# Feed-forward products of a hybrid two-block network by one level of Strassen's scheme

## The reference

```
u = _rmsnorm(h, norm_ffn_w[l])
hid = jax.nn.silu(u @ w_ffn_gate[l]) * (u @ w_ffn_up[l])      # 2048 -> 5632, twice
h = h + hid @ w_ffn_down[l]                                   # 5632 -> 2048
```

## Time and profile before

| | |
|---|---|
| median of three runs | 3690.56 us (3689.16 to 3692.22) |
| span of the profiled execution | 3688.3 us; the page gives no other time of that execution |
| TensorE busy | 3379.9 us (92%) |
| VectorE, ScalarE, GpSimd busy | 27%, 13%, 3% |
| granted TensorE clock, mean | 0.951 of full speed |
| memory traffic | 598 MB, 162 GB/s |

### The profile page before, as it was taken

One profiled execution on the slowest core, in us unless ns is written; L12 is line 12 of the kernel. 1 busy time (PEld: TensorE's weight loads), 2 busy tenths in 40 slices (PEclk: granted clock), 3 DMA queues, 4 the chain that ended last, 5 costly groups with the idle time before them and its releaser, 6 DMA issues.

```text
span 3688.3 us, 42993 instructions
## 1 busy us (share of the span) xinstructions
PE 3379.9 (92%) x17796; PEld 2888.8 (78%) x17796; DVE 1006.7 (27%) x1555; ACT 469.7 (13%) x751; POOL 126.1 (3%) x89
## 2 busy tenths in 40 slices
PE   6899998899999999889967959999899999998999
PEld 4787787788888777778856847688778888887888
DVE  5357534532310333120254741341110000001000
ACT  2114300000001222110031012211000000000000
POOL 0013300000000000010000000000000000000000
PEclk8999999899999999999977979999999999999999
DMA  9754465665554222334313332133434344342443
GB/s 411 305 213 161 183 259 242 250 250 229 228 207 154 95 102 103 114 114 159 141 65 103 114 123 94 69 133 131 165 137 151 145 159 153 143 159 100 150 156 117
DMA packets 52038, 598.39 MB, mean 162 GB/s; under 512 B 9639, under 2 KB 12214, under 8 KB 13406
## 3 DMA queue, kind: packets, MB, share of 16 engines
q1 hardware_dynamic: 51934, 596.88, 42.5%
HBM read 593.70 MB, written 3.16 MB: 162 GB/s over the span
## 4 chain that ended last, share of the span: by engine, by line
PE 74%; DVE 10%; DMA 9%; issue 2%; DVEq 2%; ACT 2%; SPq 1%; ACTq 0%; POOLq 0%; POOL 0%
PE bank L261 43%; PE bank L273 13%; PE bank L1904 8%; DMA ring<-in_t_mod 8%; DVE E L313 3%; DVE W L1584 2%; PE bank L285 2%; DVE W L1586 1%; PE bank L351 1%; PE aux L1198 1%; PE aux L1153 1%; DVE arena L1422 1%; DVE arena L313 1%; PE aux L833 0%; PE aux L1187 0%
## 5 line engine op out<-in xcount | busy, mean ns | idle before, releaser
L261 PE MATMUL bank<-hT,ring 128*128 128x256 f32 x6144 | 1343.0, 382 | 18.8 <-DVE hT L486 13.9
L261 PEld LDWEIGHTS bank<-hT,ring 128*128 128x128 f32 x6144 | 1175.7, 192 | 183.8 <-issue 20.5
L261 PE MATMUL bank<-arena,ring 128*128 128x256 f32 x3072 | 685.7, 387 | 25.7 <-DVE arena L1885 10.0
L261 PEld LDWEIGHTS bank<-arena,ring 128*128 128x128 f32 x3072 | 595.9, 194 | 112.7 <-issue 28.1
L273 PE MATMUL bank<-hT,ring 128*128 128x256 f32 x2304 | 534.9, 385 | 42.9 <-DMA ring<-in_t_ga 42.9
L273 PEld LDWEIGHTS bank<-hT,ring 128*128 128x128 f32 x2304 | 431.4, 192 | 119.0 <-issue 63.9
L1904 PE MATMUL bank<-arena,ring 128*128 128x256 f32 x1408 | 307.1, 382 | 13.1 <-DVE arena L1930 13.1
L1904 PEld LDWEIGHTS bank<-arena,ring 128*128 128x128 f32 x1408 | 269.5, 192 | 50.6 <-issue 13.5
L377 ACT ACTIVATE arena<-bank 128x512 f32 (+1 forms) x120 | 71.7, 597 | 1411.8 <-PE bank L261 1411.7
L313 DVE SCALAR_TENSOR_TENSOR E<-ring,c_act,E 128x512 f32<-128x512 f32 x240 | 180.2, 751 | 18.5 <-issue 0.6
L1930 DVE TENSOR_TENSOR arena<-arena 128x2816 f32<-128x2816 f32 x4 | 12.1, 3086 | 604.1 <-ACT arena L377 604.1
(11 more groups left out here) (335 smaller groups left out, 1977.7 us busy)
## 6 DMA issues: line engine op xcount, KB each, us to landing
ring<-in_t_mod SPq DMA_DIRECT2D x64, 2048.0 KB, 15.4
ring<-in_t_gate SPq DMA_DIRECT2D x22, 2048.0 KB, 7.7
ring<-in_t_up SPq DMA_DIRECT2D x22, 2048.0 KB, 7.7
ring<-in_t_down SPq DMA_DIRECT2D x32, 1408.0 KB, 5.9
ring<-in_t_out SPq DMA_DIRECT2D x16, 2048.0 KB, 7.8
ring<-in_t_zs SPq DMA_DIRECT2D x16, 2048.0 KB, 7.7
ring<-in_t_gdn SPq DMA_DIRECT2D x12, 2048.0 KB, 7.7
ring<-in_t_u SPq DMA_DIRECT2D x8, 2048.0 KB, 8.3
```

What stands on the lines that cost most here:

```text
L261: last = nc.tensor.matmul(bank[s][:, T * f:T * f + T], w[:, j, P * f:P * f + P], act[:, j, :], start=j == 0, stop=j == kd - 1)
```

## The change

The first two slots (one of gate, one of up) are multiplied as before. Every later gate and up slot, now loaded in turn, and every down slot are multiplied by one level of Strassen's scheme in Winograd's form: a slot's weights are taken as 2x2 blocks (even and odd contraction tile, first and second 128 output columns), the activations as 2x2 blocks (even and odd tile, first and second 128 tokens), and seven products of blocks replace eight. VectorE forms four sums of weight blocks for each slot (`dve_combos`) into one of two sets of rooms (a spare ring place, and the scratch tiles E and W), once the sums of activation blocks (`dve_halves`), and joins the seven products into four result blocks (`dve_joined`). ScalarE copies one product of each of the two banks a slot uses, since VectorE adds it to others in the same bank. Hidden tiles are formed two at a time after each up slot (`dve_hidden`), with their own block sums. The ring has three places in this part. A down product is two output tiles over 44 contraction tiles, loaded in three chunks of 8, 8 and 6 block columns. The loop bodies are six slots. The parts of the diff that matter (the removed functions stand above):

```diff
+        FRING = 3
+        FIRST_FFN = sum(n for _, n in ORDER)
+        HALF = KD // 2
+        PAIRED = KF // 2
+        CHUNKS = [(0, HALF), (HALF, HALF), (2 * HALF, PAIRED - 2 * HALF)]
+        PLAIN, GU = 2, 2 * PAIRED
+        LOOPS_GU, LOOPS_DOWN = (GU - PLAIN) // 6, HALF // 2
+        ffn_slot = [ring[:, (FIRST_FFN + k) % RING, :] for k in range(FRING)]
+        spare_slot = (FIRST_FFN + FRING) % RING
+        combo = [[ring[:, spare_slot, 1024 * q:1024 * q + 1024] for q in range(4)],
+                 [x[:, 1024 * q:1024 * q + 1024] for x in (E, W) for q in range(2)]]
...
+        h_1, h_2, h_3, h_4 = (room(3 * PAIRED * P + HALF * P * k, HALF * P) for k in range(4))
+        f_flat = w_gate[:].rearrange("p j n -> p (j n)")
+        f_up, f_two = f_flat[:, 0:512], f_flat[:, 512:640]
+        f_keep = [w_beta[:].rearrange("p j n -> p (j n)"), rstd[:]]
...
+        def weights(n, half=HALF):
+            return ffn_slot[n % FRING][:, 0:4 * half * P].rearrange("p (j a f n) -> p a f j n", a=2, f=2, n=P)
+        def sums(n, half=HALF):
+            return [x[:, 0:half * P].rearrange("p (j n) -> p j n", n=P) for x in combo[n % 2]]
+        def sp_ffn(sp):
+            def load(n, from_, half=HALF):
+                sp.dma_start(ffn_slot[n % FRING][:, 0:4 * half * P], from_).then_inc(f_in[n % FRING], 16)
+            gu, down = t["t_gu"], t["t_down"]
+            for n in range(FRING):
+                wait_old(sp, (FIRST_FFN + n) % RING)
+                load(n, gu[n])
+            with sp.Fori(0, LOOPS_GU - 1) as i:
+                for r in range(6):
+                    sp.wait_ge(f_done, 6 * i + r + 1)
+                    load(FRING + r, gu[ds(6 * i + FRING + r, 1)].rearrange("o p n -> (o p) n"))
+            for n in range(FRING + 6 * (LOOPS_GU - 1), GU):
+                sp.wait_ge(f_done, n - FRING + 1)
+                load(n, gu[n])
+            with sp.Fori(0, LOOPS_DOWN) as i:
+                for r in range(6):
+                    first, half = CHUNKS[r % 3]
+                    sp.wait_ge(f_done, 6 * i + GU + r - FRING + 1)
+                    at = slice(4 * first * P, 4 * (first + half) * P)
+                    load(GU + r, down[ds(2 * i + r // 3, 1), :, at].rearrange("o p n -> (o p) n"), half)
+        def pe_products(n, pair, half, x, halves, begins=True, ends=True):
+            w, (s1, s2, s3, s4), (x1, x2, x3, x4) = weights(n, half), sums(n, half), halves
+            first, second = bank[2 * pair], bank[2 * pair + 1]
+            for out, group in ((first, ((w[:, 0, 0], x[0][0]), (w[:, 1, 0], x[1][0]), (s2, x2))),
+                               (second, ((s1, x1), (s3, x3), (s4, x[1][1]), (w[:, 1, 1], x4)))):
+                for q, (a, b) in enumerate(group):
+                    for j in range(half):
+                        last = nc.tensor.matmul(out[:, P * q:P * q + P], a[:, j, :], b[:, j, :],
+                                                start=begins and q == 0 and j == 0, stop=ends and q == len(group) - 1 and j == half - 1)
+                if out is first and ends:
+                    last.then_inc(f_first, 1)
+            last.then_inc(f_done, 1)
+        def pe_ffn(pe):
+            for n in range(PLAIN):
+                pe.wait_ge(f_in[n], 16)
+                w = ffn_slot[n].rearrange("p (j n) -> p j n", n=SLOT_COLS)
                 for f in range(2):
...
+                    for j in range(KD):
+                        if n == 0 and f == 0 and j % QUARTER == 0:
+                            pe.wait_ge(h_ready, 16 + j // QUARTER + 1)
+                        last = nc.tensor.matmul(bank[2 * n][:, T * f:T * f + T], w[:, j, P * f:P * f + P], hT[:, j, :],
+                                                start=j == 0, stop=j == KD - 1)
+                last.then_inc(f_done, 1)
+            x = [[h_halves[:, a, h] for h in range(2)] for a in range(2)]
+            pe.wait_ge(f_halves, 1)
+            with pe.Fori(0, LOOPS_GU) as i:
+                for r in range(6):
+                    n = PLAIN + r
+                    pe.wait_ge(f_combos, 6 * i + r + 1)
+                    pe.wait_ge(f_out, 6 * i + r + 1)
+                    pe_products(n, n % 2, HALF, x, (h_1, h_2, h_3, h_4))
+            with pe.Fori(0, LOOPS_DOWN) as i:
+                for r in range(6):
+                    m, c = r // 3, r % 3
+                    first, half = CHUNKS[c]
+                    at = slice(first, first + half)
+                    pe.wait_ge(f_combos, 6 * i + GU - PLAIN + r + 1)
+                    pe.wait_ge(f_hid, first + half)
+                    if c == 0:
+                        pe.wait_ge(f_out, 2 * i + GU - 1 + m)
+                    pe_products(GU + r, m, half, [[hid_halves[:, a, h, at] for h in range(2)] for a in range(2)],
+                                (hid_1[:, at], hid_2[:, at], hid_halves[:, 0, 1, at], hid_4[:, at]), c == 0, c == 2)
+        def act_keep(act, pair, firsts, done):
+            loop_wait(act, f_first, firsts)
+            nc.scalar.copy(f_keep[pair][:, 0:P], bank[2 * pair][:, 0:P]).then_inc(f_kept, 1)
+            loop_wait(act, f_done, done)
+            nc.scalar.copy(f_keep[pair][:, P:2 * P], bank[2 * pair + 1][:, 0:P]).then_inc(f_kept, 1)
+        def act_ffn(act):
+            act.wait_ge(f_done, 1)
+            nc.scalar.activation(hid_tiles[:, 0:2, :], bank[0][:].rearrange("p (f n) -> p f n", f=2),
+                                 ACT.Silu).then_inc(f_act, 1)
+            act.wait_ge(f_done, 2)
+            nc.scalar.copy(f_up, bank[2][:]).then_inc(f_act, 1)
+            with act.Fori(0, LOOPS_GU) as i:
+                for r in range(6):
+                    n = PLAIN + r
+                    act_keep(act, n % 2, 6 * i + r + 1, 6 * i + n + 1)
+                    if r % 2 == 0:
+                        loop_wait(act, f_out, 6 * i + n + 1)
+                        nc.scalar.activation(f_gate, f_gate, ACT.Silu).then_inc(f_act, 1)
+            with act.Fori(0, LOOPS_DOWN) as i:
+                for m in range(2):
+                    act_keep(act, m, 2 * i + GU - PLAIN + m + 1, 6 * i + GU + 3 * m + 3)
+        def dve_combos(dve, n, landed, used, half=HALF):
+            v = nc.vector
+            w, (s1, s2, s3, s4) = weights(n, half), sums(n, half)
+            dve.wait_ge(f_in[n % FRING], landed)
+            if used is not None:
+                dve.wait_ge(f_done, used)
+            v.tensor_tensor(s1, w[:, 0, 1], w[:, 1, 1], ALU.add)
+            v.tensor_tensor(s3, w[:, 0, 0], w[:, 0, 1], ALU.subtract)
+            dve.drain()
+            v.tensor_tensor(s2, s1, w[:, 0, 0], ALU.subtract)
+            dve.drain()
+            v.tensor_tensor(s4, w[:, 1, 0], s2, ALU.subtract)
+            dve.drain().then_inc(f_combos, 1)
...
+        def dve_joined(dve, pair, dst, kept):
+            v = nc.vector
+            c1, c5 = f_keep[pair][:, 0:P], f_keep[pair][:, P:2 * P]
+            first, second = bank[2 * pair], bank[2 * pair + 1]
+            dve.wait_ge(f_kept, kept - 1)
+            v.tensor_tensor(dst[:, 0:P], first[:, P:2 * P], c1, ALU.add)
+            v.tensor_tensor(f_two, first[:, 2 * P:3 * P], c1, ALU.add)
+            dve.drain()
+            dve.wait_ge(f_kept, kept)
+            v.tensor_tensor(f_pair.rearrange("p (a n) -> p a n", a=2), second[:, 0:2 * P].rearrange("p (a n) -> p a n", a=2),
+                            rep(f_two, 2), ALU.add)
+            dve.drain()
+            v.tensor_tensor(dst[:, P:3 * P], second[:, 2 * P:4 * P], f_pair, ALU.add)
+            v.tensor_tensor(dst[:, 3 * P:4 * P], f_pair[:, P:2 * P], c5, ALU.add)
+            dve.drain().then_inc(f_out, 1)
+        def dve_hidden(dve, k, acts):
+            x = hid_tiles[:, ds(k * 2, 2), :] if not isinstance(k, int) else hid_tiles[:, 2 * k:2 * k + 2, :]
+            dve.wait_ge(f_act, acts)
+            gate = x if isinstance(k, int) else f_gate.rearrange("p (f n) -> p f n", f=2)
+            nc.vector.tensor_tensor(x, gate, f_up.rearrange("p (f n) -> p f n", f=2), ALU.mult)
+            dve.drain()
...
+            dve_halves(dve, [[part(a, h) for h in range(2)] for a in range(2)],
+                       one(hid_1, k), one(hid_2, k), part(0, 1), one(hid_4, k))
+            dve.drain().then_inc(f_hid, 1)
+        def dve_ffn_start(dve):
+            wait_old(dve, spare_slot)
+            dve_combos(dve, PLAIN, 16, None)
+        def dve_ffn(dve):
+            dve_halves(dve, [[h_halves[:, a, h] for h in range(2)] for a in range(2)], h_1, h_2, h_3, h_4)
+            dve.drain().then_inc(f_halves, 1)
+            dve.wait_ge(f_act, 1)
+            nc.vector.nop().then_inc(f_out, 1)
+            dve.wait_ge(f_act, 2)
+            nc.vector.nop().then_inc(f_out, 1)
+            dve_hidden(dve, 0, 2)
+            with dve.Fori(0, LOOPS_GU) as i:
+                for r in range(6):
+                    n = PLAIN + r
+                    dve_combos(dve, n + 1, 32 * i + 16 * (2 + r // 3), 6 * i + n)
```

(90 more changed lines are left out.)

6 lines of the change are left out of this document (2 added, 4 removed).

## The result

The changed kernel takes 3596.7 us (median of 4 runs, 3593.2 to 3599.3) against 3691.2 of the kernel before: ratio 0.9745, 95% interval 0.9732 to 0.9759. The forecast was 3594. Two more measurements on other occasions gave 3596.7 (0.9744, 0.9730 to 0.9757) and 3594.1 (0.9739, 0.9726 to 0.9752). The profiled execution has a span of 3593.8 us, where the forecast's sum was 3591.4, and took 3595.8 in all.

A forecast was written before the change was run, and what follows sets the result against it. TensorE's own pace was taken as the bound. Unchanged time 2753.55 + start 0.9 + first slots 30.3 + gate/up 525.4 + down 275.2 + tail 4.2 + 1.8 = 3591.4; run median 2.3 above: 3594 us, range 3583 to 3640.

The forecast's parts named there:

- The pace of a short product: TensorE's 7168 128-column MATMULs, each with its weight load: 111.7 ns each, bounds 110.7 to 118.7 and 125 ns.
- Gate, up, seam and down together: 42 gate and up slots 54.7 us less, the seam's 13.1 us gone, eight down pairs 31.9 us less.
- The seam: Gap between gate/up and down products while VectorE multiplies gate by up: its 13.1 us go.
- the down term: Down products: 2464 short MATMULs at 111.7 ns, 275.2 us for 307.1, 31.9 less.
- VectorE: Chain from one slot's end to the next sums: 9.7 us odd, 7.3 even, due after 12.5; costs nothing. Bound rival: 0.01.
- a sign: What would show the prediction: among others, VectorE busy about 16.8 us in each 25.
- The start: Slot 2's weight sums between last residual add and reciprocal delay TensorE's first gate product: cost 0.9 us.
- The tail: After TensorE's last product, copy, join and drain take 2.95 us for 1.16: 1.8 us more.
- The long run: Rival: 7168 pairs go slower than the bursts, 118.7 ns each, giving 3644 us; chance 0.15.
- The loop bodies: Rival: long bodies read again at 9 jumps, 2 to 5.9 us each, 3612 to 3647 us; chance 0.09.
- Loads on top of columns: Rival: each short product pays load plus columns, 219 ns, giving 4363 us; chance 0.03.
- The clock: Rival: TensorE's clock falls to near its lower level during short products, giving 4254 us; chance 0.01.

The follow-up runs named there:

- the experiments with 64 columns: Changed kernel with products cut to 64 activation columns, to 64 weight columns, or to both: 3594.3, 3576.8 and 3341.7 us.
- the sums moved: Changed kernel with slot 2's four weight sums put behind the scaled activations: 3591.9 us (0.9734); again, on one chip, 3591.2 against 3594.1 us.
- the 64-column kernel: Changed kernel with each Strassen product taking only the first 64 of 128 activation columns, full weight tiles: 3594.3 us.
- the third of the kernels with 64 columns: Changed kernel with each product cut to 64 weight columns against 64 activation columns: 3341.7 us.

## Why the prediction was right

*The pace of a short product*, on which all hung: put at 111.7 ns from a burst of 16, measured 111.67 over 7168. Gate, up, seam and down together were put at 99.7 us less and came to 99.8. The reason given was right too, up to which of the two is the larger. The prediction said that a pair costs the larger of load and columns; the experiments with 64 columns show that, and that it is the load by 2.5 ns. That the burst's pace held to within 0.1 ns is closer than a row of 15 gaps could promise.

*The seam* was named at 13.1 us. The 3 us of lower clock behind it were in the sum without being seen, since they lay inside the 307.1 us of the earlier trace rows that the down term was taken from.

*VectorE* was put at 9.7 us on odd and 7.3 on even slots. In the changed kernel's timeline an odd slot ends and the next starts at 2913.00 (start, duration, instruction), and the sums for the one after it end at 2922.53: 9.5 us, due after 12.5.

```profile
2913.00 3.74 PE L1967 MATMUL bank<-hT,ring 128*128 128x128 f32 x32
...
2915.91 0.29 DVE L2048 TENSOR_TENSOR arena<-arena  x1 [0.28 <-issue]
...
2921.30 1.23 DVE L2042 TENSOR_TENSOR W<-ring,E 128x1024 f32<-128x1024 f32 x1
```

Even slots took 6.9 (2900.49 to 2907.36). VectorE's busy time was 14.5 us in 25 (173.63 of 300), under the 16.8 named as a sign; that sum also held the drains, which are no busy time. The sums run at 1.22 to 1.23 us each, the contiguous row of the two that the earlier trace rows offered.

*The start* was mis-sized: 2.3 us for 0.9. The prediction started the four sums at the end of the residual add and priced them as if alone. They began 0.35 us later (2746.43 to 2746.78), and beside GpSimd's addition one of them took 2.28 us for 1.22: together the 1.4 us missed. GpSimd's addition also went from 1.26 to 1.70, and TensorE's sum of squares waits for it; but that did not count here, since ScalarE's root ended at 2751.55 and the reciprocal started only at 2752.94, behind the sums. With the sums moved all of it is gone. The Trainium skill has the rule for this on its page "SBUF — State Buffer", section "SBUF: two separate sides": a VectorE operation with two inputs in SBUF and a GpSimd operation that reads SBUF take a shared pair of ports by turns, each for a whole instruction. The trace fits that. VectorE's second sum ends at 2750.21, 1.09 us after GpSimd's addition (2749.12), which is near the 1.22 that one takes alone. GpSimd's addition in turn ends 1.11 us after VectorE's first sum (2748.01), near its own 1.26.

*The tail* was 1.1 us more for 1.8: from TensorE's end to the join's next operation it took 0.33 us (3588.53 to 3588.86) for 0.74, and the join's three operations 1.1 for 1.45.

*The rivals.* The long run has no slower pace than the burst. The loop bodies of 1344 instructions cost nothing at their jumps: the instruction queue of the changed kernel moved 5 packets from 2790 to 3300 us (10 until 3588), and its 7168 products stand without a hole.

```profile
q8 instruction: 5, 0.08, 0.1%
```

Loads on top of columns (219 ns), the rival on the slow side, is refuted over the whole run, and by the 64-column kernel in particular: were it so, half the columns would have saved 53 ns each. The clock stayed at 1.00, and VectorE held nothing; it would have from about 3 us more on an odd slot.

## What to carry to other kernels

Before trading fewer columns for more instructions, find the floor of one load and product pair in the trace, by dividing starts, not by busy over count. Here a pair with a 128x128 float32 weight tile cost 111.7 ns with 128 columns and with 64, so one level of Strassen on 256 tokens keeps three quarters of its eighth (83.6 of 110.5 us). A second level, at 64 columns a product, was not built; by the 64-column kernel each of its pairs would cost the same 111.7 ns, and there would be more of them. The other engine's chain, from the end of one slot to the deadline of the next, told the room (3 us in 12.5) better than its busy share, and must be followed through the shortest slot too. An engine made to wait may also come back at the lower clock, so that a wait costs more than its length (in the third of the kernels with 64 columns, 1.5 us more on the 32 products behind a wait of 2.9). Work that is not due for long should not be queued ahead of a chain that is due now, least of all beside an engine that it can hold up.

## What the runs showed of the hardware that was not expected

Cutting the activation columns from 128 to 64 left 7168 products at 800.38 us against 800.44: the weight load alone is the floor. An idle 13.1 us cost 3 us more behind it, at half clock. A VectorE sum of 1.22 us took 2.28 while a GpSimd addition of 1.26 took 1.70, on TensorE's critical path.
